# Sixteen more pairs of weight tiles by seven products, in the gate and attention projections

## What is computed

```python
h = rmsnorm(x, norm_mix_g)
proj = h @ w_in                      # 1024 wide input, many outputs
...
s = einsum(q, k) * dh ** -0.5 + bias # dilated window attention, 3 groups of 8 heads
p = exp(s - max(s)); l = sum(p); o = p @ v / l
y_b = sum over groups of softmax(lse) * o
...
g_a, g_b = sigmoid(gate_pre)
merged = g_a * (y_a @ w_proj_a) + g_b * (y_b @ w_proj_b)
x = x + merged @ w_out
```

## Time and profile before

| | |
|---|---|
| time, median of 3 runs | 1910.99 us (1910.97 to 1911.03) |
| span of the profiled execution, first to last instruction | 1909.1 us |
| PE busy | 1898.5 us, 99% |
| DVE, ACT, POOL busy | 1255.4 us (66%), 735.3 us (39%), 265.1 us (14%) |
| granted clock of PE | 1.00 of full speed |
| `ga` and `pa` units | about 268 to 370 us |
| attention blocks, with `qa`, `ka`, `va` and `gb` | about 370 to 614 us |

### The profile page before, as it was taken

One profiled execution on the slowest core, in us unless ns is written; L12 is line 12 of the kernel. 1 busy time (PEld: TensorE's weight loads), 2 busy tenths in 40 slices (PEclk: granted clock), 3 DMA queues, 4 the chain that ended last, 5 costly groups with the idle time before them and its releaser, 6 DMA issues.

```text
span 1909.1 us, 26308 instructions
## 1 busy us (share of the span) xinstructions
PE 1898.5 (99%) x10599; PEld 1591.0 (83%) x10599; DVE 1255.4 (66%) x1894; ACT 735.3 (39%) x1265; POOL 265.1 (14%) x156
## 2 busy tenths in 40 slices
PE   9999999999999999999999999999999999999998
PEld 7788888888888888999997778877777878899998
DVE  7777543345455748777776756766776667887874
ACT  6332322233334444344435522224444354444442
POOL 0211210111111113000004001121111133100002
PEclk9999999999999999999999999999999999999999
DMA  5322233232321323233333222322121322333332
GB/s 177 102 70 85 88 86 115 89 99 67 89 67 45 115 91 104 78 106 102 114 108 103 77 67 78 100 79 65 56 67 40 116 79 87 100 100 100 100 130 81
DMA packets 53472, 172.77 MB, mean 90 GB/s; under 512 B 5963, under 2 KB 10643, under 8 KB 53352
## 3 DMA queue, kind: packets, MB, share of 16 engines
q1 hardware_dynamic: 52912, 170.66, 28.8%
q10 hardware_dynamic: 440, 0.44, 0.1%
HBM read 168.86 MB, written 2.22 MB: 90 GB/s over the span
## 4 chain that ended last, share of the span: by engine, by line
PE 94%; DVE 3%; ACT 1%; POOL 1%; issue 0%; DVEq 0%
PE PS L1561 22%; PE PS L1563 22%; PE PS L1562 22%; PE PS L1637 5%; PE PS L1639 5%; PE PS L1638 5%; PE PS L1983 1%; PE PS L2005 1%; PE PS L1780 1%; PE PS L1795 1%; PE PS L1961 1%; PE PS L1841 1%; PE PS L1827 1%; PE PS L1818 1%; PE PS L1748 1%; POOL XT L3338 1%
## 5 line engine op out<-in xcount | busy, mean ns | idle before, releaser
L1561 PE MATMUL PS<-HH,WH 128*128 128x512 f32 x1124 | 444.0, 395 | 0.8 <-DVE WL L2467 0.7
L1563 PE MATMUL PS<-HH,WL 128*128 128x512 f32 x1124 | 438.0, 390 | 0.0
L1562 PE MATMUL PS<-HL,WH 128*128 128x512 f32 x1124 | 437.4, 389 | 0.0
L2064 ACT ACTIVATE WH<-RAW 128x1024 fp32r<-128x1024 f32 (+2 forms) x256 | 261.1, 1020 | 336.4 <-PE PS L1563 271.4
L2467 DVE TENSOR_TENSOR WL<-RAW,WH 128x1024 fp32r<-128x1024 f32 (+2 forms) x195 | 251.2, 1289 | 113.7 <-ACT WH L2064 112.0
L1561 PE MATMUL PS<-AH,WH 128*128 128x512 f32 x816 | 323.7, 397 | 0.0
L1563 PE MATMUL PS<-AH,WL 128*128 128x512 f32 x816 | 318.1, 390 | 0.0
L1562 PE MATMUL PS<-AL,WH 128*128 128x512 f32 x816 | 317.6, 389 | 0.0
L1561 PEld LDWEIGHTS PS<-HH,WH 128*128 128x128 f32 x1124 | 211.1, 188 | 49.7 <-issue 4.2
L1563 PEld LDWEIGHTS PS<-HH,WL 128*128 128x128 f32 x1124 | 211.0, 188 | 45.1
L1562 PEld LDWEIGHTS PS<-HL,WH 128*128 128x128 f32 x1124 | 211.2, 188 | 42.2 <-issue 0.2
(11 more groups left out here) (360 smaller groups left out, 2260.7 us busy)
## 6 DMA issues: line engine op xcount, KB each, us to landing
RAW<-wst SPq DMA_DIRECT2D x292, 512.0 KB, 3.6
RAW<-wst SPq DMA_DIRECT2D x16, 256.0 KB, 2.6
RAW<-wst SPq DMA_DIRECT2D x8, 384.0 KB, 3.1
XT<-xT SPq DMA_DIRECT2D x3, 512.0 KB, 7.3
out<-XT SPq DMA_DIRECT2D x4, 384.0 KB, 2.5
AR<-mx SPq DMA_DIRECT2D x4, 256.0 KB, 6.2
AR<-scr SPq DMA_DIRECT2D x16, 64.0 KB, 4.3
AR<-scr SPq DMA_DIRECT2D x8, 128.0 KB, 4.8
```

Source lines behind the costliest of these rows:

```text
L1561: T.matmul(out, wh, XH[:, k, :], start=k == 0, stop=False)
L1562: T.matmul(out, wh, XL[:, k, :], start=False, stop=False)
L1563: m = T.matmul(out, wl, XH[:, k, :], start=False, stop=k == nk - 1)
L2064: t = A.activation(whole(WH, i, n), raw(i)[:, 0:n], ACT.Copy, scale=1.0)
```

## The change

Sixteen pairs more are computed by seven products: the 8 `ga` units (4 pairs; their order becomes ga, ga, pa, pa), of the nine units of each head pair 1 to 3 the first and second, fourth and fifth, seventh and eighth (9 pairs, with single units between), and `gb` 0 and 1, 3 and 4, 6 and 7 (3 pairs). `MIXED` holds them.

- A `Stream` hands out steps: a pair is seven steps, the products in the order of `PAIR_ORDER` (0, 1, 2, 3, 4, 6, 5), a single unit four quarters. `Share` gives each block its share: 33 steps over 4 points for head pairs 0 to 2, 29 over 7 for the last. Weights are prepared as soon as the program is past the last reader of their slot.
- A pair uses three banks, `sum_z`, `sum` i and `sum` i+1; product 6 goes over product 0 in `sum_z` once ACT has kept that. In the attention `sum_z` is bank 4, and the unfolded maxima move to bank 5 (`OB`). At the end of a pair the ring is moved on by one, so the single unit behind it takes the bank of `sum` i+1, and `sum` i's goes to the pair after.
- In these pairs POOL makes all low parts of the weights and two of the four sums of weights, DVE the other two.
- DVE adds the results up (`pair_middle`, `pair_sum`) into SBUF and `pair_out` multiplies them with the norm's factor to where a single unit's eviction writes them.
- The combinations of the activations are made once, in the last two heads of the mLSTM part: `t_sums` on DVE, `t_hi` on ACT (over x itself, `TXH` lies where `XT` does), `t_lo` on POOL. x is loaded again behind the last pair (`reload_x`, 4 loads of 512 KB) and wanted by the `out` units.
- Two more raw slots, which lie in the `AL` tile, serve from the first `qa` of head pair 1 to the last `gb`.

```diff
@@ -21,6 +21,8 @@
+PAIR_ORDER = (0, 1, 2, 3, 4, 6, 5)
+ADD_ON_POOL = (5, 6)
...
-    for j in range(8):
+    for j in range(0, 8, 2):
         add("ga", j)
+        add("ga", j + 1)
         add("pa", j)
+        add("pa", j + 1)
...
+def mixed_pairs():
+    starts = [AT["ga", j, 0] for j in range(0, 8, 2)] + [AT["gb", j, 0] for j in (0, 3, 6)]
+    starts += [AT["qa", hp, 0] + x for hp in (1, 2, 3) for x in (0, 3, 6)]
+    return {p + n: p for p in starts for n in (0, 1)}
+MIXED = mixed_pairs()
...
+        if i == AT["qa", 1, 0]:
+            order += [NR, NR + 1]
+            user[NR] = user[NR + 1] = [("unit", AT["pa", 7, 0])]
+        elif i == AT["pb", 0, 0]:
+            order = [x for x in order if x < NR]
...
-            fill = Fill(e, range(at, at + n), 4 if hp < 3 else 7)
-            at += n
+            fill = Share(stream, 33, 4) if hp < 3 else Share(stream, 29, 7)
...
-    for j in range(8):
-        unit(e, unit_of("ga", j))
-        unit(e, unit_of("pa", j))
+    stream = Stream(e, unit_of("ga", 0), unit_of("gb", 7) + 1, 4)
+    for _ in range(60):
+        stream.step()
     e.ring = [0, 1]
     ask(e, 0, 0)
     e.attention_softmax(0, 0)
     e.attention_exp(0, 0)
-    attention_blocks(e)
+    attention_blocks(e, stream)
+    e.reload_x()
...
+class Stream:
+    def __init__(self, e, at, end, ready):
+        self.e, self.end, self.n = e, end, 0
+        self.steps, self.done = pair_steps(at, end, True), {}
+        for n, (kind, i, x) in enumerate(self.steps):
+            self.done[("prod", i, x) if kind == "pair" else ("unit", i)] = n
+        self.chunks = [(i, c) for i in range(at, end + 2) for c in ([None] if pair_start(i) is None else
+                                                                    PAIR_ORDER if pair_start(i) == i else [])][ready:]
+        self.n_add, self.queue = 0, []
+    def prepare(self):
+        e = self.e
+        while self.chunks and all(self.done.get(y, -1) < self.n for y in W_BEFORE[self.chunks[0]]):
+            while self.n_add < min(2, len(self.chunks)):
+                e.chunk_add(*self.chunks[self.n_add])
+                self.n_add += 1
+            self.n_add -= 1
+            y = self.chunks.pop(0)
+            e.chunk_hi(*y)
+            e.chunk_lo(*y)
+            if y[0] >= self.end:
+                break
+    def step(self):
+        e, (kind, i, x) = self.e, self.steps[self.n]
+        if kind == "pair":
+            if x == 0:
+                e.load(i + 5)
+                e.load(i + 6)
+            if x == 0 and len(e.ring) == 2:
+                e.hold(4, "sum_z", i)
+            elif x in (0, 1, 2):
+                e.sum_bank("sum" if x else "sum_z", i + (x == 2))
+            e.pair_products("1", i, x)
+        else:
+            if x[0] == 0:
+                e.load(i + 5)
+                e.sum_bank("sum", i)
+            e.products(i, x)
+        now, self.queue = self.queue, []
+        for i2, y in now:
+            e.pair_out(i2, y)
+            if UNITS[i2 + y][0] in PARTS:
+                e.later.append(("unit", i2 + y, 1))
+        self.prepare()
+        if kind == "unit":
+            if x[-1] % 4 == 3:
+                flush(e, not e.turns_apart)
+            if x[-1] == 7:
+                evict(e, i)
+        else:
+            if x in (1, 3, 4, 5):
+                flush(e, not e.turns_apart)
+            if x == 0:
+                e.pair_keep(i)
+            elif x == 6:
+                e.pair_middle(i)
+            if x in (6, 5):
+                e.pair_sum(i, int(x == 6))
+                self.queue.append((i, int(x == 6)))
+            if x == 5 and len(e.ring) == 2:
+                e.taken += 1
+        self.n += 1
+    def finish(self):
+        e = self.e
+        for i2, y in self.queue:
+            e.pair_out(i2, y)
+            if UNITS[i2 + y][0] in PARTS:
+                e.later.append(("unit", i2 + y, 1))
+        self.queue = []
+        self.prepare()
+        while self.chunks:
+            self.n += 1
+            self.prepare()
...
+        SPARE = [plain("AL", j, 1024, use="raw") for j in (4, 6)]
+        def temps(i):
+            if i not in MIXED:
+                return KEPT, HELD, GATE if UNITS[i][0][0] == "g" else [UP, UP]
+            t = GA_TEMPS if UNITS[i][0] == "ga" else AT_TEMPS
+            return t[0], t[1], t[2:4]
...
+            def reload_x(s):
+                sp.wait_ge(*at("prod", unit_of("gb", 6), 6))
+                for g in range(4):
+                    d = S.dma_start(XT[:, 2 * g:2 * g + 2, :], xT_d[:, 2 * g:2 * g + 2, :])
+                    d.then_inc(*x_back[g].next("x_back", g))
...
-                          4: (("sum_z", i), 256), 5: (("sum", i), 256), 6: (("sum_w", i), 0)}[c]
+                          4: (("sum_z", i), 256), 5: (("sum", i), 256),
+                          6: (("sum_z" if i in MIXED else "sum_w", i), 0)}[c]
                 out = PS[:, s.bank[key], o:o + 256]
-                if c in (0, 1, 2, 6):
+                if c in (0, 1, 2) or c == 6 and i not in MIXED:
                     s.free(*key)
-                elif c == 4:
+                elif c in (4, 6):
                     pe.wait_ge(*at("kept", i))
                 pe.wait_ge(*at("lo", i, c))
                 wh, wl = chunk(WH, i, c), chunk(WL, i, c)
+                if sfx == "1":
+                    for m in range(4):
+                        pe.wait_ge(*at("t_lo", m))
+                        w, k = slice(128 * m, 128 * m + 128), m + 4 * (c in (1, 3, 4, 5))
+                        x = slice(256, 512) if c in (2, 3, 5) else slice(0, 256)
+                        XH, XL = (HH, HL) if c in (0, 1, 5) else (TXH, TXL)
+                        T.matmul(out, wh[:, w], XH[:, k, x], start=m == 0, stop=False)
+                        T.matmul(out, wh[:, w], XL[:, k, x], start=False, stop=False)
+                        t = T.matmul(out, wl[:, w], XH[:, k, x], start=False, stop=m == 3)
+                    t.then_inc(*unit_sum.next("prod", i, c))
+                    return
...
-                t = T.matmul(PS[:, 4, 0:64], con("unfold"), strips, start=True, stop=True)
+                t = T.matmul(PS[:, OB, 0:64], con("unfold"), strips, start=True, stop=True)
...
+            def t_hi(s, m):
+                act.wait_ge(*at("t_sums", m))
+                act.wait_ge(*at("gates", "sum"))
+                t = A.activation(TXH[:, m:m + 5:4, :], T_SUM.rearrange("p (x t) -> p x t", x=2), ACT.Copy, scale=1.0)
+                t.then_inc(*act_done["attn"].next("t_hi", m))
...
+            def pair_middle(s, i):
+                kept, held, _ = temps(i)
+                z = PS[:, s.bank["sum_z", i], :]
+                dve.wait_ge(*at("prod", i, 6))
+                dve.wait_ge(*at("kept", i))
+                V.tensor_tensor(held[:, 0:256], z[:, 256:512], kept[:, 0:256], ALU.add).then_inc(
+                    *dve_done["attn"].next("held", i))
+                dve.wait_ge(*at("held", i))
+                t = V.tensor_tensor(held[:, 256:512], z[:, 0:256], held[:, 0:256], ALU.add)
+                t.then_inc(*bank_read.next("free", "sum_z", i))
+            def pair_sum(s, i, n):
+                kept, held, outs = temps(i)
+                out, src = outs[n], PS[:, s.bank["sum", i + n], :]
+                if n:
+                    dve.wait_ge(*at("free", "sum_z", i))
+                    h = held[:, 256:512]
+                    twice = bass.AP(h.tensor, h.offset, [list(h.ap[0]), [0, 2], [1, 256]])
+                    V.tensor_tensor(kept[:, 256:512], src[:, 256:512], held[:, 0:256], ALU.add).then_inc(
+                        *dve_done["attn"].next("kept_2", i))
+                    t = V.tensor_tensor(out.rearrange("p (x t) -> p x t", x=2), src.rearrange("p (x t) -> p x t", x=2),
+                                        twice, ALU.add)
+                else:
+                    dve.wait_ge(*at("prod", i, 5))
+                    dve.wait_ge(*at("kept_2", i))
+                    t = V.tensor_tensor(out, src, kept, ALU.add)
+                t.then_inc(*bank_read.next("free", "sum", i + n))
...
+            def t_sums(s, m):
+                A_, B_ = T_IN
+                T1, T4, T5, T6 = (T_SUM[:, 256 * n:256 * n + 256] for n in range(4))
+                if m:
+                    dve.wait_ge(*at("t_sums", m - 1))
+                V.tensor_scalar(A_, XT[:, m, :], col("mix_g", m), None, ALU.mult, ALU.bypass)
+                t = V.tensor_scalar(B_, XT[:, m + 4, :], col("mix_g", m + 4), None, ALU.mult, ALU.bypass)
+                t.then_inc(*dve_done["attn"].next("t_x", m))
+                dve.wait_ge(*at("t_x", m))
+                if m:
+                    dve.wait_ge(*at("t_lo", m - 1))
+                V.tensor_tensor(T1, B_[:, 256:512], A_[:, 256:512], ALU.subtract)
+                t = V.tensor_tensor(T4, A_[:, 256:512], A_[:, 0:256], ALU.subtract)
+                t.then_inc(*dve_done["attn"].next("t_1", m))
+                dve.wait_ge(*at("t_1", m))
```

(33 more changed lines are left out.)

146 lines of the change are left out of this document (116 added, 30 removed).

## The result

The changed kernel takes 1944.88 us (median of four runs, 1943.67 to 1946.23), the kernel before, beside it on the same chip, 1911.01 (1910.97 to 1911.27): a ratio of 1.0177 [1.0165, 1.0190], 33.9 us slower. The sign of the forecast was right. The size was not: 10.1 us were forecast, and the time lies 13.9 us above the range. The profiled execution has a span of 1941.8 us, 32.7 more than that of before.

The account below looks back on a forecast made before the run. PE was taken to bound the kernel as a dense chain of matmuls. Gains of 15.7 us against 25.8 us of waits gave +10.1 on a span of 1909.1, so 1919.2 and a time of 1921.0 us; 8-in-10 range 1906 to 1931.

Parts of the forecast that it names:

- What the products give back: All 16 new pairs: seven products instead of two single units gain 0.98 us each, 15.7 us in all.
- The handover of a bank: Behind twelve attention pairs PE waits for DVE to free the single unit's bank: 0.92 us each, 8.3 us for nine.
- rival (1): All hidden: the single unit's bank is free in time, nothing stands, all 15.7 us stay, 1895.3 us; chance 0.10.
- Where the end of a pair meets an attention block: DVE's queue behind two merges costs PE 4.6 us twice, 9.3 us; late weights in the first `gb` pair cost 4.0.
- Weights in time: POOL's low parts come late at pair starts behind cuts, 2.1 us plus 1.5; no wait in the `ga` part.
- The first attention pair: Behind the first scores, low parts of weights come late: about 2.1 us of PE standing, with two restarts.
- the three others: Three other pairs starting just behind a cut: 0.5 us of waiting each, 1.5 us together.
- Two users of one SBUF: POOL and DVE meeting in SBUF costs either 0.45 us, mostly off the path; nothing added to the sum.
- Rival (3): POOL and DVE block one another: twelve pairs lose 0.7 to 1.4 us more each, 1929 to 1938 us; chance 0.12.
- The matmuls on `TXH` ... 0: Matmuls on `TXH` have the feed-forward pairs' shape, starts 0.118 us apart, so no added cost: 0.
- (2): Only the handovers cost, 11.0 us against 15.7: 1906.3 us, up to 1913 with pair starts or one merge; chance 0.18.
- the sign of (3): In the profile after, PE's waits for POOL would come in every pair.

## Why the prediction was right in sign and wrong in size

- *"What the products give back"*: right, -15.3 for -15.7, and with it the thought that a wait of 1 us behind a pair takes its gain away.
- *"The handover of a bank"*: right. The chain of four additions measured 0.68 us for the last and 0.42 for the three before, the wait 0.76 in place of 0.92 (once 1.20): the term was 1.1 us too large. The attempt to lengthen its cover shifted the wait to POOL. So a shorter handover alone would not have brought rival (1): a second limit lies behind it, which the forecast did not name.
- *"Where the end of a pair meets an attention block"*: right in mechanism and size, 4.36 for 4.6 twice and 3.6 for 4.0. The first two are shown by moving `rest_yb`, the third by other cuts, which took `unfold` out from in front of the weights. What it left out is what a wait of that length does behind it.
- *"Weights in time"* failed in its last sentence, "In the `ga` part ... no wait". The low parts were counted, the loads were not: the twelve bias loads in front of the second pair's weights on SP were in the trace of before, and a change that takes weights earlier had to be followed through that queue. 5.1 us in waits; moving the loads took 5.5 off the time, the half clock behind the wait in it. The first attention pair was 1.2 for 2.1, the three others nothing.
- *"Two users of one SBUF"* failed: "nothing is added to the sum". The rows showed 0.45 us for a meeting, and I took this for the price of each. The 1.13 us of the earlier trace rows are of another operation than the 0.69 beside it, one that alone takes 0.75. It ended 0.55 us after the POOL instruction that it had met, just as L2734 did above: the rows fit two engines that take turns, and what a meeting costs depends on how much of the other's instruction is left. At POOL's new share of the time (71 us to 245 busy between 200 and 700), instructions begin in the middle of POOL's and stand till its end, small ones too. The turns lost 4.5 us in waits, and `unfold` cost 1.95 for 0.6; for the two largest turns the rows give the whole wait, for the others a part. No run took the meetings away and left the work where it was. The Trainium skill, SBUF — State Buffer, section "Who interferes with whom", says that the later of the two blocks fully, and its rule takes in `tensor_scalar`; 0.42 to 2.60, 0.175 to 1.20 and 0.69 to 1.75 us here agree with it. The forecast set this rule aside for the rows that it had picked; but the trace of before also held 0.75 to 2.90 us (L2734, above), which agrees with the rule and not with 0.45. Rival (3) had the mechanism with a price of 0.7 to 1.4 on each of twelve pairs; measured it is at most some 6 us, at six waits, since most meetings fall on work off the path.
- *The clock was in no sum.* Behind each of the four waits of 3.3 us and more PE runs at 1.2 GHz for some 3 to 4 us, and once behind three shorter ones: 6.6 us in all, nearly as much as the nine handovers. Filling two of the waits with matmuls brought the clock back to 1.00, so the cause is shown. The Trainium skill, TensorE: Matmul & The Clock Gate, section "HAM oscillation — how this bites in real kernels", warns that PE standing idle between groups of matmuls brings its clock down; the rows above agree. The forecast itself counted three such waits (4.6, 4.6, 4.0), so this was there to be seen.
- *"The matmuls on `TXH` ... 0"* failed: 0.1198 us where the feed-forward pairs have 0.1179, some 2.5 us in 1344 matmuls. Those that read `HH` have 0.1198 as well. The shape is the same and the distance is not; the cause was not found.
- *The end of the stretch* had no term, 2.5 us: 0.77 for the second `pair_sum` of the last pair, 0.45 for a low part of POOL, 1.30 for a low part of the activations on DVE (L2660), which works 63 us more between 200 and 700. Why the last comes late was not followed.
- *The rivals.* (1) and (2) fell: no handover was hidden, and all else was not free. Nor did POOL's waits come in every pair, the sign of (3). What came about were the forecast's own mechanisms, (3)'s in part, and two that stood in no case, the loads and the clock.

So the step that failed is the list of terms put at nothing: loads in the `ga` part (5.1 us measured), two users of one SBUF (4.5 and 1.35), the distance of the matmuls (2.5), and the clock, for which there was no term (6.6). The six costs that it had priced came to 22.6 for 25.8. 4.4 us stay in small distances that were not traced.

The range was too narrow since its upper end held only one rival. SBUF and the loads could each have had an upper bound from the trace of before; together with the clock they were larger than the 10.1 us that it added up to.

## What to carry to other kernels

Where an edit trades PE time for work on three other engines, price the waits with their aftermath: four waits of 3.3 to 4.2 us here cost about a third as much again at the lower clock (5.2 us behind 15.1 us of waits). Before you put a zero beside a queue, read in the trace what stands in it just ahead of the new instruction: here a dozen small loads on SP, and on DVE an operation that waits for ACT's exponentials. And when POOL and DVE both add from SBUF, take the whole of the other's instruction as the price of a meeting and ask which of them are on the path; a gain of 1 us a pair bears none.
